# Requests for cache pages, release of key buffers, and the order of scale and copy in two attention stages

## The reference

```python
# prompt, query block i of 128 positions, keys up to its end
s = (einsum('bqhn,bkhn->bhqk', qn, k_nope) + einsum('bqhr,bkr->bhqk', qr, k_rope)) * scale
s = where(key_pos[None, :] <= q_pos[:, None], s, -inf)
p = softmax(s, axis=-1)
o = einsum('bhqk,bkhv->bqhv', p, v)

# samples, over pages of the cache that a page table names
ckv_past = cache_ckv[l, page_table].reshape(db, past_len, KV_LORA)      # 8 x 8192 x 256
kr_past  = cache_krope[l, page_table].reshape(db, past_len, MLA_ROPE)   # 8 x 8192 x 32
s = concat([einsum('bthl,bpl->bhtp', q_lat, ckv_past) + einsum('bthr,bpr->bhtp', q_rope, kr_past), s_new]) * scale
p = softmax(s)
lat = einsum('bhtp,bpl->bthl', p[..., :P], ckv_past) + einsum('bhts,bsl->bthl', p[..., P:], c_kv)
```

## Time and profile before

| | us |
|---|---|
| median of 3 runs | 1910.0 |
| lowest, highest | 1909.35, 1912.11 |
| profiled execution | 1910.69 |
| its span, first to last instruction | 1908.8 |
| TensorE matmuls busy | 1827.8 (96%) |
| VectorE busy | 1216.4 (64%) |
| ScalarE busy | 569.3 (30%) |
| GpSimd busy | 567.0 (30%) |
| mean granted TensorE clock | 0.987 |

### The profile page before, as it was taken

One profiled execution on the slowest core, in us unless ns is written; L12 is line 12 of the kernel. 1 busy time (PEld: TensorE's weight loads), 2 busy tenths in 40 slices (PEclk: granted clock), 3 DMA queues, 4 the chain that ended last, 5 costly groups with the idle time before them and its releaser, 6 DMA issues.

```text
span 1908.8 us, 34292 instructions
## 1 busy us (share of the span) xinstructions
PE 1827.8 (96%) x14782; PEld 1587.6 (83%) x14782; DVE 1216.4 (64%) x1563; ACT 569.3 (30%) x978; POOL 567.0 (30%) x392
## 2 busy tenths in 40 slices
PE   7999999898998999989998899999999999999998
PEld 6989889885664444449997699999999999999998
DVE  5587776565877887874332756873675276375475
ACT  5222321353553454452121531120111021011026
POOL 2222122240001343422224533333332333333530
PEclk9999999998999999999999999999999999999999
DMA  7121122141002888853134511112111211211202
GB/s 245 45 57 45 47 57 45 39 123 48 1 1 91 324 320 314 315 188 104 30 89 143 177 56 45 46 39 61 45 41 42 63 39 34 61 45 43 79 23 92
DMA packets 162307, 176.72 MB, mean 93 GB/s; under 512 B 21982, under 2 KB 146932, under 8 KB 157772
## 3 DMA queue, kind: packets, MB, share of 16 engines
q1 hardware_dynamic: 146240, 93.54, 16.7%
q0 software_dynamic: 7168, 75.50, 10.5%
q10 hardware_dynamic: 8750, 5.49, 1.0%
HBM read 161.33 MB, written 13.27 MB: 91 GB/s over the span
## 4 chain that ended last, share of the span: by engine, by line
PE 87%; DVE 7%; issue 3%; ACT 1%; DMA 1%; POOL 1%; SPq 0%; ACTq 0%; DVEq 0%; POOLq 0%
PE PS L799 21%; PE PS L801 20%; PE PS L800 20%; PE PS L1120 4%; PE PS L836 4%; PE PS L1162 3%; PE PS L1014 2%; PE PS L1107 1%; PE PS L1142 1%; PE PS L1055 1%; PE PS L1131 1%; PE PS L881 1%; PE PS L987 1%; PE PS L1335 1%; PE PS L1337 1%
## 5 line engine op out<-in xcount | busy, mean ns | idle before, releaser
L737 POOL CAST whi<-wraw 128x1024 fp32r<-128x1024 f32 (+4 forms) x142 | 137.4, 968 | 915.8 <-PE PS L801 860.0
L799 PE MATMUL PS<-BH,whi 128*128 128x344 f32 x1152 | 368.9, 320 | 0.0
L800 PE MATMUL PS<-BL,whi 128*128 128x344 f32 x1152 | 367.1, 319 | 0.0
L801 PE MATMUL PS<-BH,wlo 128*128 128x344 f32 x1152 | 367.0, 319 | 0.0
L739 POOL TENSOR_TENSOR wlo<-wraw,whi 128x1024 fp32r<-128x1024 f32 (+4 forms) x142 | 311.2, 2192 | 11.4
L800 PEld LDWEIGHTS PS<-BL,whi 128*128 128x128 f32 x1152 | 216.2, 188 | 0.5 <-issue 0.5
L799 PEld LDWEIGHTS PS<-BH,whi 128*128 128x128 f32 x1152 | 216.2, 188 | 0.5 <-issue 0.5
L801 PEld LDWEIGHTS PS<-BH,wlo 128*128 128x128 f32 x1152 | 216.2, 188 | 0.0
L799 PE MATMUL PS<-XH,whi 128*128 128x344 f32 x528 | 179.0, 339 | 3.4 <-DVE XL L1911 3.4
L2391 DVE TENSOR_TENSOR XT<-PS,XT 128x1032 f32<-128x1032 f32 x48 | 59.2, 1233 | 175.9 <-PE PS L801 175.8
L800 PE MATMUL PS<-XL,whi 128*128 128x344 f32 x528 | 170.1, 322 | 0.0
(11 more groups left out here) (451 smaller groups left out, 3713.5 us busy)
## 6 DMA issues: line engine op xcount, KB each, us to landing
wraw<-in_w_up_dram SPq DMA_DIRECT2D x44, 512.0 KB, 3.9
wraw<-in_w_in_dram SPq DMA_DIRECT2D x20, 512.0 KB, 4.0
wraw<-in_w_down_dram SPq DMA_DIRECT2D x24, 256.0 KB, 2.9
wraw<-in_w_down_dram SPq DMA_DIRECT2D x16, 320.0 KB, 3.3
xt_kept<-XT SPq DMA_DIRECT2D x1, 4128.0 KB, 12.8
XT<-xt_kept SPq DMA_DIRECT2D x1, 4128.0 KB, 13.9
xstage<-in_x_prompt_dram SPq DMA_DIRECT2D x8, 512.0 KB, 10.4
wraw<-in_w_out_dram SPq DMA_DIRECT2D x8, 512.0 KB, 4.2
```

What stands on the lines that cost most here:

```text
L737: gp.tensor_copy(hi, raw).then_inc(w_hi_done, 1)
L799: pe.matmul(out, wh[:, t, 0:m], hi[:, tile(t), s], start=(t == first), stop=False)
L800: pe.matmul(out, wh[:, t, 0:m], low, start=False, stop=False)
L801: ins = pe.matmul(out, wl[:, t, 0:m], hi[:, tile(t), s], start=False, stop=(t == last))
```

## The change

Four edits. In `load_pages` a request for group g also waits for the first half of group g - 4's turned weights, that is until that group's values can begin. In GpSimd's loop the values of a sequence are weighed and added ahead of the request of the same turn, not behind it. The semaphore `kp_used` is gone: key pairs 1 to 3 of a group wait until TensorE has ended all scores of the group before. In prompt attention the scale of unit n + 1 stands ahead of the copy of unit n's turned weights.

```diff
@@ -752,6 +752,7 @@
                     full(gp, ("po", len(units) - 1))
                 elif g >= SLOTS:
                     full(gp, ("go", g - SLOTS))
+                    gp.wait_ge(half_turned, g - SLOTS + 2)
                 at_ = bass.IndirectOffsetOnAxis(ap=idx[:, g:g + 1].bitcast(U32), axis=0)
@@ -767,10 +768,10 @@
                 if j == job_no[("out", 0)]:
                     for g in range(SLOTS + GT - NG):
+                        if g >= SLOTS and (g - SLOTS) % NG == NG - 1:
+                            sequence_values(gp, step, (g - SLOTS) // NG)
                         if g < GT:
                             load_pages(g)
-                        if g >= SLOTS and (g - SLOTS) % NG == NG - 1:
-                            sequence_values(gp, step, (g - SLOTS) // NG)
@@ -1119,8 +1120,6 @@
                                         tile_position=(32 * r, j))
-                    if s in (2, 4, 6):
-                        ins.then_inc(kp_used, 1)
                 if g:
                     turn_weights(g - 1)
@@ -2247,6 +2246,8 @@
                 if n + 2 < len(units):
                     softmax_max(n + 2)
+                if n + 1 < len(units):
+                    softmax_scale(n + 1)
                 if q >= 2:
                     key = ("pt", n, 1)
                     full(ve, key)
@@ -2254,8 +2255,6 @@
                         full(ve, ("po", values_before(n)))
                     m = q + 1 if n < PAIRS else q - 3
                     take(ve.tensor_copy(turned(n)[:, 4:4 + m, :].rearrange("p m q -> p (m q)"), bank(key)[:, 0:m * P]))
-                if n + 1 < len(units):
-                    softmax_scale(n + 1)
@@ -2290,10 +2289,7 @@
             def turn_key_pair(g, n):
                 before = 4 * g + n - KSLOTS
                 if before >= 0:
-                    if before % 4 == 3:
-                        full(ve, ("pp", before // 4, 1))
-                    else:
-                        ve.wait_ge(kp_used, 3 * (before // 4) + before % 4 + 1)
+                    full(ve, ("pp", before // 4, 1))
                 if n == 3:
                     turn_last_slice(g, 0)
                     return
```

More of the change, by code:

```diff
@@ L241, in build_program @@
         xt_out, xt_back = sem("xt_out"), sem("xt_back")
-        part_zero, kr_turned, kp_turned, kp_used, half_turned = [sem(n) for n in ("part_zero", "kr_turned", "kp_turned", "kp_used", "half_turned")]
+        part_zero, kr_turned, kp_turned, half_turned = [sem(n) for n in ("part_zero", "kr_turned", "kp_turned", "half_turned")]
         g_max, seq_w, seq_wd, seq_l, seq_o = sem("g_max"), sem("seq_w"), sem("seq_wd"), sem("seq_l"), sem("seq_o")
```

## The result

| | before | after |
|---|---|---|
| median of 4 runs each, us | 1909.67 | 1892.83 |
| lowest, highest | 1908.47, 1912.11 | 1891.35, 1895.4 |
| span of the profiled execution | 1908.8 | 1889.5 |
| scores of group 0 begin at | 609.29 | 601.59 |
| scores of group 0 to scores of group 31 | 233.4 | 224.1 |

The span is 19.3 us shorter. Up to the first scores of paged attention it lost 7.7 us, close to the forecast of 7.5. Paged attention, forecast at nothing, lost 9.3 us (233.4 against 224.1). The other 2.3 us lie behind it; there the kernel before has one stretch more with a granted clock of 0.50, at about 1096 us.

What follows compares the result with a forecast made beforehand. TensorE was taken as the bound: by its own work in paged attention, partly waiting for VectorE's scaling in prompt attention. Terms 5.4 + 0.5 + 1.6 = 7.5 us, paged attention nothing, gave 1902.5 us by the median; range 1899.5 to 1907.0.

Steps and rivals of the forecast that it cites:

- Nothing but TensorE's own work can shorten it.: Paged attention: TensorE is busy 59.38 of 60 us, so the only question is whether a new wait gets past its cover.
- Cost nothing: Paged attention: page requests go out 5.1 us later, but pages still land in time; no cost.
- rival (d): Paged attention: pages come late and hold VectorE's keys, then TensorE, in 27 groups; 1916.0 us at a 13.6 us landing; 6%.
- the paged period still 7.5 us: Sign of being right: paged attention keeps its pace of one group every 7.5 us.
- Nothing is held: Paged attention: sequence values ahead of a request end at 713.5, before the request's wait ends at 714.4; no delay.
- Release of key buffers: Paged attention: 96 increments removed, gain taken as 0, at most 2.5 us; VectorE's later key pairs cost nothing.
- Rival (b): Paged attention: the removed semaphore increments did cost time; 2.5 us more gain, 1900.0 us; 7%.
- The cover named for VectorE: Paged attention: 1.9 us before TensorE takes ScalarE's exponential hides VectorE's later maximum; without it 3 us lost.
- The swap: Prompt attention: scaling ahead of the copy shortens TensorE's waits; 5.4 us, plus 0.5 us for blocks 2 and 3.
- Rival (c): Prompt attention: the bank takes most of the swap's gain, no clock gain, 1906.5 us, 8%; or no change, 9%.
- The clock: End of prompt attention: the last gap shrinks to 1.55 us, so TensorE's clock stays up; 1.6 us gained.
- Rival (a): End of prompt attention: the clock still falls behind the last gap, or falls elsewhere; 1904.1 us; 20%.

Runs made afterwards that it cites:

- e2: The kernel before with only the key buffers released once a group, 96 increments fewer; ratio 1.0009 (0.999 to 1.0028).
- e6: The changed kernel with pages loaded by SyncE's plain DMAs in memory order instead of GpSimd's indirect requests; one run, 1875.0 us.
- e7: The changed kernel with pages loaded for the first five groups alone, later groups reusing them; one run, 1878.62 us.

## Why the prediction failed, point by point

**"Nothing but TensorE's own work can shorten it."** This is the step that failed. The prediction took the busy share (59.38 of 60 us) and the period of 7.5 us as TensorE's own pace. Matmul ends are modelled, so an engine whose instructions start sparsely still looks busy. What the runs showed in its place: GpSimd's requests stretched TensorE's scores of each group by 1.25 us (3.49 against 2.24), and moving them away shortened the stage by 9.3 us with TensorE's own work unchanged. The row that would have spoken, 2.51 against 1.29 us for the same 44 matmuls, stood in the trace of before, in the last four groups; only one group from the middle was read the earlier trace rows.

**Requests.** "Cost nothing" was half right: pages are not late (no wait of VectorE for them in the changed kernel), so rival (d) didn't come, and the delay was 5 us as worked out. But only their price when late had been asked for, not what they cost TensorE where they stood: 1.25 us a group. The later request takes 0.57 of it back in ordinary groups (3.49 - 2.92) and more where a gap holds the scores back; of 18.6 us in the scores 8.7 go to the new gaps, and 9.3 are left over the stage. The term was set at nothing, with a loss as its only other case; a gain was never priced. Of its signs of being right, "the paged period still 7.5 us" is the one that failed: 6.95.

**Sequence values ahead.** "Nothing is held" holds for the order as changed, and so the reorder was costed at nothing. It is what makes the later request pay: with the old order the changed kernel takes 13 us more. The prediction never asked what the wait would do to the operations queued behind it on GpSimd in the old order, which would have told what the reorder is there for.

**Release of key buffers.** Right: nothing that can be told, twice measured (1.0009; 0.9911 against 0.9916). Rival (b), and the 26 ns an increment that the Trainium skill gives (TensorE: Matmul & The Clock Gate, "The cost: per-tile semaphore tail"), by which the estimate was 2.5 us, are not borne out: e2's interval reaches down to 1.9 us of gain, its value is a loss of 1.7, and the 0.02 us a group by which the scores are shorter come to some 7 ns an increment. The cover named for VectorE was there at 7 us a group; at 6.27 it is gone once in four groups in e6 and e7.

**The swap.** Right: 5.4 + 0.5 = 5.9 us forecast, 6.3 (3.6 to 8.8) measured alone, and 5.3 + 0.3 us turn by turn in the traces. By blocks 4 to 7 the forecast was 1.1, 1.6, 1.8 and 1.2 us, less 0.3, and 0.8, 1.3, 1.8 and 1.4 came. Rival (c), the bank, is there with 0.5 us over the stretch instead of the 2.4 us that it was allowed. The remaining gap was forecast at 1.55 us and is 1.64.

**The clock.** The 1.6 us were there in the changed kernel's trace and not in that of the swap alone, behind gaps of the same length. Rival (a) had this at 20%; with one row at 1.45 us as the only ground, that the forecast came true was luck, and half of the term, as an even chance, would have been the honest one.

**The sum.** 7.5 us were forecast up to paged attention, and 7.7 came, of which 7.1 are the forecast's own terms (5.6 and 1.5); the rest is what was left of a lead from before the first edit. The miss is the 9.3 us of paged attention, a term set to 0 with no bound on the gain beyond the 2.5 us of idle time.

## What to carry to other kernels

Before calling a stage bound by its own work, compare the same instructions in its first and last groups with the middle ones: a busy engine can be a slowed one, and what is absent at the edges (here GpSimd's requests) is the suspect. Make GpSimd's indirect requests beside matmuls that they don't slow (here the values), not beside a dense run like these scores, and look at what is queued behind the wait that puts them there. Two edits that are worth nothing alone (1.0013 and 1.0009) are worth 0.5% together here (0.9916 / 0.9967 = 0.9949, with the release, which gives nothing).

## What the runs showed of the hardware

- An indirect DMA that GpSimd requests costs TensorE up to 1.2 us where it meets a dense run of score matmuls (44 take 1.29 us without, 2.51 with one of the pair ahead of the scores and one inside, 3.7 with both inside), still 0.7 us where the second of the pair ends 0.1 us into the scores, and nothing beside the values (32 in 1.93 us with and without). Plain DMAs of SyncE with the same bytes cost nothing (1.27 us), nor does indirect traffic at 437 GB/s once it has been requested (1.27 us), nor GpSimd's arithmetic (1.29 us beside L713 to L715). By what way a request slows TensorE no run shows; that stays open.
- TensorE stops for 0.3 to 1.8 us at some of a row of places 125 or 126 matmuls apart, and goes on 1.2 to 1.6 us behind the landing of a 16 KB packet on the instruction queue. In the run without pages there is no such gap within the values.
- After gaps of 1.63 and 1.64 us at the same place of the program the granted clock was once 0.50 and once 1.00.
